# Two edits to a one-core hybrid Hyena and pooling encoder layer: the gated rows' middle tap on ScalarE, and the input's first pieces asked for ahead of the filter stage's stores

## What is computed

```python
u = x * (1 + scale) + shift                       # scale, shift, gate from silu(c) @ w_ada + b_ada
proj = u @ w_in + b_in                            # 1024 -> 3072 columns
hy_streams, hy_gate, pool_in, pool_gate = split(proj)
s = short_conv(hy_streams)                        # three taps along the tokens, per channel, with a bias
v, x1, x2 = split(s)                              # 512 channels each
z = x1 * long_conv(v, k[0]);  z = x2 * long_conv(z, k[1])     # two filters of length 2L, by FFT over 2L
y_h = z * silu(hy_gate)
y_p = pooled(pool_in) * silu(pool_gate)           # windows 2, 4, 8, 16, per-group map
out = gate * (concat(y_h, y_p) @ w_out + b_out)
return layer_norm(alpha * x + out)
```

## Time and profile before

| | |
|---|---|
| median of 3 runs (range) | 1197.19 us (1195.09 to 1198.83) |
| the profiled execution | 1202.5 us, of it 1200.7 us span from first to last instruction |
| granted clock, mean over the span | 0.962 |
| PE, DVE, ACT, POOL busy | 1099.5, 857.5, 577.2, 12.6 us |
| moved by DMA | 273.24 MB, mean 228 GB/s |

### The profile page before, as it was taken

The page is one execution under the profiler, slowest core; times in us unless marked ns, Lnnn a source line. Parts: engine busy times, 40 slices in busy tenths (PEclk is TensorE's granted clock), DMA queues, the critical chain, the costliest instruction groups (busy, mean ns, idle before and its releaser), DMA issues. The chain is left out here.

```text
span 1200.7 us, 14193 instructions
## 1 busy us (share of the span) xinstructions
PE 1099.5 (92%) x4928; PEld 846.2 (70%) x4928; DVE 857.5 (71%) x1093; ACT 577.2 (48%) x757; POOL 12.6 (1%) x32
## 2 busy tenths in 40 slices
PE   3799679999999999989999999897999769999995
PEld 0268567888888877767887877665788557888883
DVE  6589776555545545639999756554999967888878
ACT  4068683444535354527777534432787863221210
POOL 0001000000000000000000000000000000000000
PEclk8789979999999999999999999999999889999998
DMA  9948954677775536587999578768799999556321
GB/s 348 306 144 298 377 194 158 193 235 244 228 255 174 197 99 200 205 253 229 296 277 281 159 228 264 243 216 237 216 296 274 295 343 309 163 194 199 134 88 53
DMA packets 155132, 273.24 MB, mean 228 GB/s; under 512 B 11503, under 2 KB 49519, under 8 KB 153396
## 3 DMA queue, kind: packets, MB, share of 16 engines
q1 hardware_dynamic: 151605, 266.74, 69.4%
q0 software_dynamic: 3168, 5.51, 2.1%
q10 hardware_dynamic: 288, 0.08, 0.0%
HBM read 178.95 MB, written 98.57 MB: 231 GB/s over the span
## 5 line engine op out<-in xcount | busy, mean ns | idle before, releaser
L177 PE MATMUL u_pp<-uh_uhi,prj_whi 128*128 128x512 f32 x768 | 311.0, 405 | 16.6 <-DVE u_ulo L745 10.5
L178 PE MATMUL u_pp<-u_ulo,prj_whi 128*128 128x512 f32 x768 | 306.1, 399 | 0.0
L179 PE MATMUL u_pp<-uh_uhi,prj_wlo 128*128 128x512 f32 x768 | 305.7, 398 | 0.0
L177 PEld LDWEIGHTS u_pp<-uh_uhi,prj_whi 128*128 128x128 f32 x768 | 146.8, 191 | 59.0 <-issue 15.3
L179 PEld LDWEIGHTS u_pp<-uh_uhi,prj_wlo 128*128 128x128 f32 x768 | 146.6, 191 | 34.8
L178 PEld LDWEIGHTS u_pp<-u_ulo,prj_whi 128*128 128x128 f32 x768 | 147.0, 191 | 32.8
L1260 DVE TENSOR_TENSOR p_alo<-xin_pair,p_ahi 128x1024 fp32r<-128x1024 f32 x32 | 39.2, 1226 | 101.0 <-ACT p_ahi L1197 101.0
L1197 ACT ACTIVATE p_ahi<-xin_pair 128x1024 fp32r<-128x1024 f32 x32 | 33.9, 1061 | 126.9 <-PE p_ps L179 119.3
L558 PE MATMUL fs_s<-fs_khi,flt_tab 64*128 64x512 f32 x256 | 51.9, 426 | 5.5 <-ACT prj_cv L602 3.1
L2199 ACT ACTIVATE p_sm<-p_mv,p_eps 128x1 f32<-128x1 f32 x16 | 4.7, 296 | 107.9 <-DVE p_mv L2290 107.9
L597 ACT ACTIVATE fs_khi<-fs_k 128x1024 fp32r<-128x1024 f32 x32 | 33.9, 1060 | 44.1 <-DVE fs_k L574 44.1
(11 more groups left out here) (210 smaller groups left out, 2119.0 us busy)
## 6 DMA issues: line engine op xcount, KB each, us to landing
xin_pair<-kseq SPq DMA_DIRECT2D x32, 512.0 KB, 4.4
kfreq<-xin_pair SPq DMA_DIRECT2D x32, 512.0 KB, 5.2
xseq<-p_xo SPq DMA_DIRECT2D x32, 512.0 KB, 7.5
p_k_re<-kfreq SPq DMA_DIRECT2D x64, 256.0 KB, 5.7
p_k_im<-kfreq SPq DMA_DIRECT2D x64, 256.0 KB, 4.8
bseq<-p_out SPq DMA_DIRECT2D x32, 512.0 KB, 5.0
prj_ws<-in_t_win SPq DMA_DIRECT2D x24, 512.0 KB
kseq<-prj_row SPq DMA_DIRECT2D x22, 512.0 KB, 4.7
```

What stands on the lines that cost most here:

```text
L177: nc.tensor.matmul(out, w[0], m[0], start=start, stop=False, skip_group_check=True)
L178: nc.tensor.matmul(out, w[0], m[1], start=False, stop=False, skip_group_check=True)
L179: return nc.tensor.matmul(out, w[1], m[0], start=False, stop=stop, skip_group_check=True)
```

## The change

In fs1, SP issues the eight pieces of x, the first weight column and the constants before its first wait, instead of one at a time after the stores of units 18 to 27. In `Gated`, for pairs 1 to 3 (12 chunks), ACT writes `cv = row * w[1] + b` right after it has written the row (`centre`), and DVE adds the two side taps (`sides`): the same scalar_tensor_tensor twice, and the tensor_scalar that began the convolution is gone. The wait for the gate that read `cv` before moves from DVE to ACT. The other 36 convolutions (v, x1 and pair 0) stay as they are.

```diff
         def _(sp):
+            for m in range(8):
+                pj.load_x(sp, m)
+            pj.load_w(sp, 0)
+            pj.load_consts(sp)
             for n in range(N):
                 sp.wait_ge(evac_done[n % 2], n // 2 + 1)
                 sp.dma_start(group_rows(kseq[n % 2], fl.group(n // 2)), xo[n % 3]).then_inc(stored[n % 3], 16)
-                if n == N - 14:
-                    pj.load_w(sp, 0)
-                if N - 13 <= n < N - 9:
-                    pj.load_x(sp, n - (N - 13))
-                if n == N - 9:
-                    pj.load_consts(sp)
-                if N - 8 <= n < N - 4:
-                    pj.load_x(sp, n - (N - 12))
@@ class Gated: from_bank
         super().from_bank(act, q)
+        if not self.is_gate(q) and self.pair(q):
+            self.centre(act, q)
+
+    def centre(self, act, q):
+        pj, c, tile = self.pj, q % 4, TILES[q // 4]
+        pj.was_read(act, q)
+        act.wait_ge(self.gated[c % 2], 2 * self.pair(q) - 1 + c // 2)
+        self.nc.scalar.activation(pj.cv[:, c * CH:(c + 1) * CH], pj.row[:, PAD + c * CH:PAD + (c + 1) * CH], ACT.Identity,
+                                  scale=pj.cw[:, 1, tile:tile + 1], bias=pj.cb[:, tile:tile + 1]).then_inc(self.centred, 1)
+
+    def sides(self, dve, q):
+        pj, c, tile = self.pj, q % 4, TILES[q // 4]
+        cv = pj.cv[:, c * CH:(c + 1) * CH]
+        done = 2 * (4 * convs_before(q // 4) + c)
+        pj.row_ready(dve, q)
+        dve.wait_ge(self.centred, 4 * (self.pair(q) - 1) + c + 1)
+        for i, sem in ((0, pj.conv_step), (2, pj.row_used)):
+            if i:
+                dve.wait_ge(pj.conv_step, done + 2)
+            self.nc.vector.scalar_tensor_tensor(out=cv, in0=pj.row[:, PAD - 1 + i + c * CH:PAD - 1 + i + (c + 1) * CH],
+                                                scalar=pj.cw[:, i, tile:tile + 1], in1=cv, op0=ALU.mult,
+                                                op1=ALU.add).then_inc(sem, 1 if i else 2)
@@ class Gated: post
             if self.pair(q):
-                dve.wait_ge(self.gated[q % 2], 2 * self.pair(q) - 1 + q % 4 // 2)
-            self.pj.conv(dve, q)
+                self.sides(dve, q)
+            else:
+                self.pj.conv(dve, q)
```

More of the change, by code:

```diff
@@ L923, with __init__ @@
 class Gated(Pairs):
+    def __init__(self, nc, s, pj, first, base):
+        super().__init__(nc, s, pj, first, base)
+        self.centred = s.sem("centred")
     def product(self, c):
```

## The result

The changed kernel takes 1186.8 us (median of 7 runs, 1182.6 to 1190.0) against 1198.8 us of the kernel before on the same chip (7 runs). The ratio is 0.9888, with a 95% interval of 0.9867 to 0.9909: 13.4 us less, with 10.9 to 15.9 as the interval (the two medians alone are 12.0 us apart). On the 1197.2 us of the prediction that is 1183.8 us. The profiled execution took 1187.7 us, with a span of 1185.8.

The account below looks back on a forecast made before the run. PE was taken as full in p1 to p3 and the tail, late store landings as stalling fs1's end, DVE as pacing p5. Terms 5.8 + 0.5 + 1.5 = 7.8 us took 1197.2 to 1189.4 us, range 1186.5 to 1194.5.

Parts of the forecast that it names:

- Head priced at 0: Start of fs1: the early requests delay nobody, as a backlog until 74.5 us costs nothing; 0 us, upper bound 1 us.
- The rival of a collision there: Start of fs1: requests run slower than 298 GB/s and the first stores land late; 1192.9 us, chance 0.08.
- the one of stores that are slow by themselves: End of fs1: late stalls stay even without x, leaving only 2.0 us of gain; 1195.2 us, chance 0.08.
- The stage's end: End of fs1: stalls for stores go and the last copy comes 5.3 to 6.1 us earlier; taken as 5.8 us.
- p4, 0.5 us: p4: PE waits less for `xlow` as DVE loses a TENSOR_SCALAR; between 0 and 0.7 us, taken as 0.5.
- p5, 1.5 us: p5: DVE's saving shortens PE's waits at the first `inv`, three convolution steps and step 13; taken as 1.5 us.
- the 0.5 us of the forecast: p5, three convolution steps after the first `inv`: they run at PE's 8.36 us instead of DVE's 8.53; 0.5 us.
- the 1.1 us of the prediction: p5's end, step 13: the gap between `fwd` ending at 943.4 us and `straight` beginning at 944.53 can go; 1.1 us.
- the loss by a late `yhigh`: p5: `yhigh` behind the centre on ACT becomes late and may show in each step; 7 x 0.1 = 0.7 us lost.
- the hold by full transfers: p5: transfers at 412 GB/s and a share of 1.03 may hold the stage's end, which gives 0 gain.
- its bound of 2.1: p5: the most it could gain, 1.0 us in the earlier steps plus 1.1 us at the stage's end.
- ACT as the engine waited for (1201.0 us): The 12 centre steps, before `xhigh` or `evac` and `yhigh`: 0.80 us each, 9.6 in full, 3.8 slower overall; chance 0.05.

Follow-up runs that it names:

- experiment 2: Kernel before unedited: 1199.4 us. Changed kernel plus one redundant DVE wait in p4: 1188.9. Early requests alone plus redundant waits, seven DVE instructions more: 1191.5.

## Why the prediction was right in direction and too small

By the stages of the profiles with and without each piece, the change is worth 7.2 (fs1) + 0.6 (p4, not to be told from its spread) + 2.1 (way) + 2.4 (p5) = 12.3 us, against 13.4 [10.9, 15.9] and 12.1 [7.2, 17.0] in the two comparisons. The forecast was 5.8 + 0.5 + 0 + 1.5 = 7.8. Of the 4.5 us that it lacks, 2.1 were a term that it put at nothing (the way), 1.4 a landing that was sized too long (fs1), and 0.9 a term taken too far below its own bound (p5).

- **Head priced at 0: right.** The transfers ran at 387 and 396 GB/s, the first stores were issued without a wait, and no copy before 120 us waited for a landing. The rival of a collision there falls, and so does the one of stores that are slow by themselves.
- **The stage's end: right mechanism, one size off.** The last window multiplication was forecast at 133.9 and the copy of unit 28 at 137.1 us. Less the 0.75 us by which this execution began the stage earlier, that is 133.15 and 136.35; measured are 133.20 and 136.36. The step that failed is "its store is issued at 138.1 and lands 4.4 to 5.3 us later, which frees the buffer for the last copy at 142.6 to 143.4". That buffer was free before 140.61 us, at most 3.3 us after its copy ended at 137.36. The landings were read from rows 4, in a stretch where stores and tables kept the queue at 0.88. The store of unit 28 is issued into a queue that has emptied: from 136 to 138 us the share is 0.41 at 149 GB/s (second row from the end of the first fence). That this is why it landed sooner is likely, but no run tests it alone. Tile `prj_row`, stores from 134 to 146 us of the changed kernel, issue to landing:

```profile
DMA to landing us min/median/max: 3.1/3.9/4.7
```

With the landing no longer what the last copy waits for, PE is, and 5.8 should have been 7.2.

- **p4, 0.5 us: not contradicted.** With the tap p4 lasts 117.1 to 117.7 us, without it 117.0 to 119.9 (means 117.4 and 118.0).
- **The way from p4 to p5: a term that was missing.** The prediction went from p4 to p5 without a word on what lies between, and so put it at nothing; it is 2.1 us, has nothing to do with the work that was moved, and so is luck. Shown is that it follows DVE's instruction count: experiment 2 sets it to 10.9 and to 8.8 us by waits alone. It reaches PE, too: PE's waits for the first low halves (`p_alo`) in p5 sum to 1.6 to 3.4 us in the seven profiles with the fetch at that place and to at most 1.1 in the others. That the fetch itself delays one of the load's sixteen shares is inferred from the late increment. The Trainium skill, "DMA: Bandwidth & Descriptors", Queues, rings and completion order, says that row 14 serves the runtime's refills and that each DMA engine takes turns between its rows. The q14 record beside the late share fits that; the taking of turns itself no run here shows.
- **p5, 1.5 us: right mechanism, taken too low.** PE and not DVE tells what p5 gained. The first product of `fwd` on PE in steps 2 and 5, in the kernel before and then in the changed one:

```profile
849.29 0.40 PE L177 MATMUL p_u<-p_ahi,p_fwd 128*128 128x512 f32 x1
...
874.88 0.40 PE L177 MATMUL p_u<-p_ahi,p_fwd 128*128 128x512 f32 x1
```
```profile
836.54 0.40 PE L177 MATMUL p_u<-p_ahi,p_fwd 128*128 128x512 f32 x1
...
861.64 0.39 PE L177 MATMUL p_u<-p_ahi,p_fwd 128*128 128x512 f32 x1
```

The three steps took 25.59 us, 8.53 each, and take 25.10, 8.37 each. So DVE's pace is no longer what holds them, PE's own is, and the 0.5 us of the forecast came. DVE's steps of 8.0 us are no gain of their own: DVE was behind and catches up, with `straight` 3.72 us behind its `fwd` in step 2 (840.26 - 836.54) and 1.28 us in step 13 (929.83 - 928.55). Then its gate steps, too, last PE's 8.36 us. The other two places are `inv` in step 1, which waited 1.40 us for `ylow`, and `inv` in step 13. Here is step 1 in the changed kernel, then step 13 in the kernel before and in the changed one:

```profile
832.24 0.50 PE L177 MATMUL p_b<-p_yhi,p_inv 128*128 128x512 f32 x1 [0.82 <-DVE p_ylo L1684]
```
```profile
944.49 0.50 PE L177 MATMUL p_b<-p_yhi,p_inv 128*128 128x512 f32 x1 [1.17 <-DVE p_ylo L1662]
```
```profile
929.93 0.39 PE L177 MATMUL p_b<-p_yhi,p_inv 128*128 128x512 f32 x1
```

The first wait is 0.58 us shorter, where 0.54 was said. The wait in step 13 is gone, as the 1.1 us of the prediction had it; the next step gives 0.3 back, so `fwd` of step 15 follows that of step 13 after 12.33 us instead of 13.13. Together 0.6 + 0.5 + 0.8 = 1.9 us. What lies between that and the 2.4 of the table can't be told from the spread of p5 (144.1 to 145.3 us in the profiles without a centre there). The term that was mis-sized is "I take 1.5": neither the loss by a late `yhigh` nor the hold by full transfers, for which it went below its bound of 2.1, shows in these rows.

- **ACT as the engine waited for (1201.0 us): out**, by the change and by the doubled centre, which costs 1.9 us where 9.6 would be the full price. Yet the place was named rightly: it is `yhigh` behind the centre, and one more activation showed in full in half of the steps. The rule cited from the Trainium skill ("ScalarE: Activation LUTs", Rules for kernel authors) holds for the instruction, 0.82 against 0.54 us, and misleads where VectorE holds up PE and ScalarE has room.
- **What would show it.** Rate at the head, last window, 36 TENSOR_SCALARs, 0.82 us a centre: as said. p1 began 8.1 us earlier instead of 5.8 (0.75 of it stood before the stage). The convolution steps of 8.4 us in p5 came on PE; DVE's own take 8.0 while it catches up.

## What to carry to other kernels

Put loads for a later stage where the queue stands still, not merely earlier: among the stores of a stage whose engine has no gap, the same requests cost their stall wherever they are. Read what a shorter step is worth on the engine that sets the pace: DVE's steps became 0.54 us shorter each, while PE's went only from 8.53 to 8.37 us. And cut the stages of several profiles at the same instructions before explaining a gain: a place that changed by 2 us though its work did not may only have had its instruction fetch moved, and the next edit may move it back.

## What the runs showed of the hardware

- The records have fetches of instructions of 8 KB each on a DMA queue of their own. With one of them 1.1 us behind a 512 KB load, the load took 5.4 to 6.0 us from request to use (seven profiles), without it 3.5 to 3.7 (six), and one DVE instruction more or less decided whether it fell there. It cost 2.1 us where this one load was what everything waited for; what the other fetches cost, no run shows.
- Stores and strided loads together moved 382 GB/s at a share of 1.05, and the same loads alone 387 to 396 GB/s. Mixed with them, the stores came late and the stage was 6.1 us longer than with the loads ahead of them.
- An ACTIVATE with scale and bias per partition took 0.819 us on 128x512 as the centre, 0.802 as the form it was priced by the earlier trace rows.
